# Order of work in the first attention stage of a two-block layer: projections as filling, gates and pa's products moved

## The reference, cut to what matters

```python
z = h @ w_in                      # fq fk fv ff dq dk dv ga gb
log_f = log_sigmoid(ff + b_fgate)
o_a = fox_attention(fq, fk, fv, log_f)        # 8 heads of 64, causal, bias F_q - F_k (F = cumsum(log_f))
o_b = rms_norm(diff_attention(dq, dk, dv))    # 4 heads: softmax(q1 k1) - lam * softmax(q2 k2), v of 128
y = sigmoid(ga + b) * (o_a @ w_pa) + sigmoid(gb + b) * (o_b @ w_pb)
x = x + y @ w_o
```

## Time and profile before

| | |
|---|---|
| median of three runs | 1101.2 us (1100.53 to 1102.28) |
| profiled execution: its own time | 1100.98 us |
| its span, first to last instruction | 1099.2 us |
| mean granted TensorE clock | 0.965 of 2.4 GHz |
| busy: PE, DVE, ACT, POOL | 93%, 36%, 34%, 13% of the span |
| first block's mixer, until the last matmul of wo1 | to about 254 us |
| routing and experts | to about 760 us |
| second block | to the end |

### The profile page before, as it was taken

The page is one execution under the profiler, slowest core; times in us unless marked ns, Lnnn a source line. Parts: engine busy times, 40 slices in busy tenths (PEclk is TensorE's granted clock), DMA queues, the critical chain, the costliest instruction groups (busy, mean ns, idle before and its releaser), DMA issues.

```text
span 1099.2 us, 14880 instructions
## 1 busy us (share of the span) xinstructions
PE 1019.1 (93%) x6333; PEld 713.8 (65%) x6333; DVE 391.3 (36%) x753; ACT 370.7 (34%) x610; POOL 138.1 (13%) x87
## 2 busy tenths in 40 slices
PE   7999999887999999998989999886999999999996
PEld 6996779866544444433334333335898999999995
DVE  3444335454312121211111101214433443683464
ACT  5444555543011111111111111014345564655342
POOL 1110011322000000000000000001312102242123
PEclk8998999889999999999999999898899999999999
DMA  8964666347599999999999999996264554554400
GB/s 294 345 240 151 230 220 249 146 180 306 188 421 420 419 420 420 419 418 421 419 419 420 419 419 419 419 404 229 90 216 169 176 175 154 187 179 172 173 1 38
DMA packets 83003, 307.92 MB, mean 280 GB/s; under 512 B 6607, under 2 KB 11112, under 8 KB 58352
## 3 DMA queue, kind: packets, MB, share of 16 engines
q1 hardware_dynamic: 79144, 302.16, 70.2%
q10 hardware_dynamic: 3784, 4.73, 1.3%
HBM read 305.81 MB, written 2.63 MB: 281 GB/s over the span
## 4 chain that ended last, share of the span: by engine, by line
PE 71%; DMA 10%; DVE 7%; SPq 4%; ACT 4%; issue 2%; POOL 1%; ACTq 0%; POOLq 0%; DVEq 0%
PE bank L722 69%; DMA arena<-in_w 5%; DMA ring<-in_w 5%; SPq L774 4%; DVE arena L1184 2%; DVE arena L1187 2%; DVE arena L1190 1%; DVE wR L1184 1%; PE bank L1133 1%; ACT wR L1732 1%; ACT arena L1903 1%; POOL wR L2067 1%; PE bank L906 1%; PE bank L900 0%; POOL small L2055 0%
## 5 line engine op out<-in xcount | busy, mean ns | idle before, releaser
L722 PE MATMUL bank<-hTR,wR 128*128 128x256 f32 x2520 | 316.6, 287 | 5.1 <-DVE wR L1184 2.0
L722 PEld LDWEIGHTS bank<-hTR,wR 128*128 128x128 f32 x2520 | 309.1, 194 | 8.7 <-issue 7.2
L722 PE MATMUL bank<-ring,arena 128*64 128x512 f32 (+1 forms) x1056 | 228.7, 602 | 9.5 <-DMA ring<-in_w 9.4
L1732 ACT ACTIVATE wR<-ring 128x1024 fp32r<-128x1024 f32 x161 | 168.2, 1053 | 119.2 <-PE bank L722 117.2
L1184 DVE TENSOR_TENSOR wR<-ring,wR 128x1024 fp32r<-128x1024 f32 x121 | 153.0, 1271 | 151.6 <-ACT wR L1732 151.4
L722 PE MATMUL bank<-arena 128*64 128x512 f32 (+8 forms) x778 | 171.8, 549 | 12.3 <-DMA arena<-in_w 6.3
L722 PEld LDWEIGHTS bank<-ring,arena 128*64 128x64 f32 (+1 forms) x1056 | 69.3, 136 | 141.9 <-issue 129.0
L2067 POOL TENSOR_TENSOR wR<-ring,wR 128x1024 fp32r<-128x1024 f32 x40 | 97.3, 2431 | 387.3 <-ACT wR L1732 387.3
L1184 DVE TENSOR_TENSOR arena<-arena,bank 128x256 f32<-128x256 f32 (+1 forms) x36 | 16.0, 450 | 363.7 <-ACT arena L1903 358.1
L1882 ACT ACTIVATE arena<-bank 64x512 f32<-64x512 f32 x64 | 37.9, 593 | 307.9 <-PE bank L722 307.5
L722 PEld LDWEIGHTS bank<-arena 128*64 128x64 f32 (+4 forms) x778 | 67.4, 154 | 100.2 <-issue 82.8
(11 more groups left out here) (204 smaller groups left out, 846.8 us busy)
## 6 DMA issues: line engine op xcount, KB each, us to landing
ring<-in_w SPq DMA_DIRECT2D x120, 1024.0 KB, 25.1
arena<-in_w SPq DMA_DIRECT2D x72, 1024.0 KB, 25.5
ring<-in_w_in SPq DMA_DIRECT2D x30, 2048.0 KB, 8.9
ring<-in_w_ada SPq DMA_DIRECT2D x6, 2048.0 KB, 8.0
ring<-in_w_o SPq DMA_DIRECT2D x2, 2048.0 KB, 11.6
ring<-in_w_o_attn SPq DMA_DIRECT2D x2, 2048.0 KB, 7.8
ring<-in_w_o_conv SPq DMA_DIRECT2D x2, 2048.0 KB, 7.8
ring<-in_w_out SPq DMA_DIRECT2D x2, 2048.0 KB, 9.1
```

The costliest lines, as they stand in the source:

```text
L722: return pe.e.matmul(o, l, r, start=start, stop=stop)
L1732: eng.activation(h, w, ACT.Copy).then_inc(s_high, 1)
```

## The change

- dq and dk go into the filling: dq's two halves are drawn from it before the loop (the first, then `cumsum`, then the second), dk in rounds 0 and 1, dv in rounds 2 and 3.
- Only `bf` 0 stands in front of the loop. `bf` 1, 2 and 3 are in rounds 0, 2 and 4, behind that round's `qk`.
- `ada` i stands in the filling in front of gate projection i, 4 and 5 behind g3. Every round takes two units of filling until round 15; it runs out there. The order of loads is changed to fit (g1 before ada2, and so on).
- pa's four pieces leave the filling: they run in rounds 16 and 17 and behind the loop, among the last differential head's steps. Their gates are made beside them.
- pa's product is no longer copied from PSUM by ACT and multiplied by POOL: DVE multiplies bank and gate into `PA` in one instruction. The sigmoids of all four quarters stand in front of the pb loop.
- `outer_pe` waits for each head's output at the first product that reads it, not for all four in front.

```diff
-        chunks += [ada[0], gate[0], ada[1], ada[2], gate[1], ada[3], gate[2], ada[4], gate[3], ada[5]]
+        chunks += [ada[0], gate[0], ada[1], gate[1], ada[2], gate[2], ada[3], gate[3], ada[4], ada[5]]
...
-        project(O1, "dq", "h1")
-        PB.use("zT", 7)
-        PB.use("cum", 7)
-        O1.add("cumsum")
-        project(O1, "dk", "h1")
-        O1.add("rbuf")
-        for hp in range(4):
-            PB.use(("bf", hp), SR.next())
-            O1.add("bf", hp)

         def fill_first():
+            for nm in ("dq", "dk"):
+                for c2 in range(2):
+                    u = PB.use((nm, c2), PR.next())
+                    for st in O1.pair(nm, c2, u, "h1"):
+                        O1.add(*st)
+                        if st[3] == 0:
+                            yield
+                    O1.add("evict", nm, c2)
+                    yield
...
+            def ada_step(i):
+                u = PB.use(("adaw", i), PR.next())
+                O1.add("ada", i)
+                O1.loads.release(f"ada{i}")
+                yield
+                PB.use(("ada", i), u.bank)
+                O1.add("ada_sum", i)
+
             for g in range(4):
+                yield from ada_step(g)
                 for c2 in range(2):
...
-            for jj in range(4):
-                u = PB.use(("pa", jj), PR.next())
-                i_ = O1.take("pa")
-                done_by(i_, u)
-                O1.add("outer", i_, "pa", jj)
-                O1.add("evict", "pa", jj)
-                yield
+            for i in (4, 5):
+                yield from ada_step(i)
...
         fill = fill_first()
+        for _ in range(2):
+            next(fill)
+        PB.use("zT", 7)
+        PB.use("cum", 7)
+        O1.add("cumsum")
+        for _ in range(2):
+            next(fill)
+        O1.add("rbuf")
+        PB.use(("bf", 0), SR.next())
+        O1.add("bf", 0)
...
-            ada_sum()
-            next(fill, None)
-            if i in (0, 4, 5, 7, 9, 12):
-                ada_step()
+            if i < 6 and i % 2 == 0:
+                PB.use(("bf", i // 2 + 1), SR.next())
+                O1.add("bf", i // 2 + 1)
+            if i < 16:
+                next(fill, None)
+            elif i == 16:
+                for _ in fill:
+                    pass
+                pa_outer(0)
             if job:
                 PB.use(("pt", n_pt), TR.next())
                 O1.add("p_turn", n_pt, *job)
...
-            if i in (6, 9, 11, 12, 13, 14, 15):
+            if i < 16:
                 next(fill, None)
-        while late:
-            next(fill, None)
-            h = late.pop(0)
-            PB.use(("dt", h), U_["do", h].bank)
-            O1.add("diff_turn", h)
-        for _ in fill:
-            pass
+            elif i == 16:
+                O1.add("gate", 0)
+                O1.add("evict", "pa", 0)
+                pa_outer(1)
+        O1.add("gate", 1)
+        O1.add("evict", "pa", 1)
+        pa_outer(2)
+        PB.use(("dt", 3), U_["do", 3].bank)
+        O1.add("diff_turn", 3)
+        O1.add("gate", 2)
+        O1.add("evict", "pa", 2)
+        pa_outer(3)
+        O1.add("gate", 3)
+        O1.add("evict", "pa", 3)
         for jj in range(4):
-            O1.add("gate", jj)
             u = PB.use(("pb", jj), PR.next())
...
-            for m in range(4):
-                emptied(pe, U_["fo" if nm == "pa" else "dt", m])
             for s in range(2):
                 for k in range(4):
+                    emptied(pe, U_["fo" if nm == "pa" else "dt", k])
...
+                    elif nm == "pa":
+                        u = U_["pa", c2]
+                        filled(v, u)
+                        v.wait_ge(s_gate, c2 + 1)
+                        emptied(v, U_["s", 7])
+                        tt(flat2(PA, 2 * c2), banks[u.bank][:, :], flat2(gates, 2 * c2), ALU.mult).then_inc(u.free, 1)
...
-                        eng.activation(flat2(PA, 2 * c2), banks[u.bank][:, :], ACT.Copy).then_inc(u.free, 1)
...
-                    eng.tensor_tensor(flat2(PA, 2 * jj), flat2(PA, 2 * jj), flat2(gates, 2 * jj), ALU.mult).then_inc(s_pag, 1)
```

More of the change, by code:

```diff
@@ L362, in bass_two_hybrid_blocks @@
                              "drs", "dsq"))
-        s_siluc, s_gate, s_pag, s_ysum, s_yh, s_shift, s_rexp, s_ss, s_rrow, s_rbuf, s_sca = (
-            sem(n) for n in ("siluc", "gate", "pag", "ysum", "yh", "shift", "rexp", "ss", "rrow", "rbuf", "sca"))
+        s_siluc, s_gate, s_ysum, s_yh, s_shift, s_rexp, s_ss, s_rrow, s_rbuf, s_sca = (
+            sem(n) for n in ("siluc", "gate", "ysum", "yh", "shift", "rexp", "ss", "rrow", "rbuf", "sca"))
         s_gA, s_ag, s_aTh, s_uz, s_conv, s_cb, s_cg, s_cTh, s_msum, s_mh, s_fg = (
@@ L496, in fill_first, with pa_outer @@
                     yield
-            for jj in range(4):
-                u = PB.use(("pa", jj), PR.next())
-                i_ = O1.take("pa")
-                done_by(i_, u)
-                O1.add("outer", i_, "pa", jj)
-                O1.add("evict", "pa", jj)
-                yield
-        fill = fill_first()
[L506 to L521, removed]
+            for i in (4, 5):
+                yield from ada_step(i)
+        def pa_outer(jj):
+            u = PB.use(("pa", jj), PR.next())
+            i_ = O1.take("pa")
+            done_by(i_, u)
+            O1.add("outer", i_, "pa", jj)
+        fill = fill_first()
+        for _ in range(2):
[8 more added lines that the diff above has]
+        O1.add("bf", 0)
         late, out_of = [], []
@@ L566, in bass_two_hybrid_blocks @@
                 n_pt += 1
-            if i in (6, 9, 11, 12, 13, 14, 15):
+            if i < 16:
                 next(fill, None)
-        while late:
-            next(fill, None)
-            h = late.pop(0)
-            PB.use(("dt", h), U_["do", h].bank)
-            O1.add("diff_turn", h)
-        for _ in fill:
-            pass
+            elif i == 16:
[7 more added lines that the diff above has]
+        O1.add("diff_turn", 3)
+        assert late == [3] and not out_of
+        O1.add("gate", 2)
[3 more added lines that the diff above has]
+        O1.add("evict", "pa", 3)
         for jj in range(4):
-            O1.add("gate", jj)
             u = PB.use(("pb", jj), PR.next())
@@ L584, in bass_two_hybrid_blocks @@
         O1.add("y", 3)
-        assert ada_next[0] == 6 and not ada_full
         O1.add("x_again")
@@ L1349, in first_steps @@
                     emptied(v, u)
-                    v.wait_ge(s_pag, jj + 1)
+                    emptied(v, U_["pa", jj])
                     tt(T, T, flat2(PA, 2 * jj), ALU.add).then_inc(s_ysum, 1)
@@ L1770, in first_steps @@
                         last.then_inc(u.free, 1)
-                    elif nm == "pa":
-                        u = U_["pa", c2]
-                        filled(s, u)
-                        emptied(s, U_["s", 7])
-                        eng.activation(flat2(PA, 2 * c2), banks[u.bank][:, :], ACT.Copy).then_inc(u.free, 1)
                 elif what == "ada":
@@ L2078, in first_steps @@
                     rsqrt(st[:, 4:6], st[:, 2:4], s_drs)
-                elif what == "gate":
-                    jj = a[0]
-                    emptied(p, U_["pa", jj])
-                    p.wait_ge(s_gate, jj + 1)
-                    eng.tensor_tensor(flat2(PA, 2 * jj), flat2(PA, 2 * jj), flat2(gates, 2 * jj), ALU.mult).then_inc(s_pag, 1)
             def second_norm():
```

## The result

The changed kernel takes 1092.19 us (median of 6 runs, 1091.67 to 1095.31), the kernel before 1101.41 on the same chip (6 runs, 1098.67 to 1103.02): ratio 0.9925, 95% interval [0.9907, 0.9943]. That is about 9 us faster by the medians and 8.3 by the ratio (6.3 to 10.2 by its interval). The forecast was 1.4, and its range ended at 1094.5. The profiled execution took 1091.67 us for a span of 1089.9, at a mean granted clock of 0.972.

The account below looks back on a forecast made before the run. Loads bound the expert stage, whose start waits for PE through the mixer. A gain of 0.9 us until the first pb product ended plus net 0.5 behind it made 1.4: 1099.8 us, range 1094.5 to 1105.

Parts of the forecast that it names:

- The bound of the stage: Expert stage: DMA at full share, 1.01 at 416 GB/s, so it lasts as long as its bytes take.
- So whatever the mixer gains or loses passes to the end one for one: From the first expert's refill at 283.46 on: the refill waits for PE, so mixer gains reach the end unchanged.
- The waits of the mixer: PE's idle time up to the first pb product: 9.4 us in the new order against 10.6 before.
- Clock in the mixer: Low clock up to the first pb product: round 0 certain at 2.6; cumsum, rounds 4 and 16 together 4.0 us.
- From the first pb product to wo0: Chain from that product's end to wo0's third piece: 19.4 us instead of 22.1, without sigmoids and POOL's multiplications.
- The low clock at wo0: At the start of wo0's third piece: clock low after PE idles, costing 2.2 us ahead of 72 matmuls without a wait.
- Sum of the mixer: Whole mixer: 0.9 gained until the first pb product has ended, net 0.5 from there, together 1.4 us.
- The rule of the table load: ACT's sigmoid table load: 1.28 us by the row; the skill's added 1.38 drain would make the gain 0.5, not 1.4.
- Exchange: Mixer, the forecast itself: waits and clock give back nearly what goes, 1099.8 us (1098 to 1102.5); chance 0.42.
- The clock holds: Cumsum, round 4 and round 16 keep 2.4 GHz, 4.0 us come back: 1095 to 1096 us; chance 0.34.
- DVE held up: Loop rounds 11, 13, 15: PE waits on DVE's splits queued behind POOL's rsqrt, 1104.5 to 1106 us; chance 0.2.
- the loads decide: In the loop: a chunk comes late, each 2 MB taking about 5 us; chance 0.04, to either side.

Follow-up runs that it names:

- d_before: Kernel before with eleven identity matmuls, about 2.3 us, added in front of the first expert: 1099.29 us, ratio 0.9988.
- k_before: Kernel before with 6 and 4 identity matmuls that end inside PE's waits at the end of the expert stage: 1095.52 us, ratio 0.9945.
- k_after: Changed kernel with 6 and 4 identity matmuls that end inside PE's waits at the end of the expert stage: 1092.89 us, ratio 0.9925.
- d_after: Changed kernel with eleven identity matmuls, about 2.3 us, added in front of the first expert: 1096.43 us, ratio 0.9955.
- h_after: Changed kernel with 13 and 9 identity matmuls at PE's waits in experts 28 to 31, longer than those waits: 1100.14 us, ratio 1.0004.
- h_: Kernel before and changed kernel, each with 13 and 9 identity matmuls at PE's waits in experts 28 to 31: 1104.01 and 1100.14 us.
- d_: Kernel before and changed kernel, each with eleven identity matmuls in front of the first expert: 1099.29 and 1096.43 us.
- k_: Kernel before and changed kernel, each with 6 and 4 identity matmuls inside waits late in the expert stage: 1095.52 and 1092.89 us.
- The held pair: Kernel before and changed kernel, each with 6 and 4 identity matmuls inside waits late in the expert stage: ratios 0.9945 and 0.9925.
- the three edits: Changed kernel with cumsum behind dq's third tile, `bf` 3 in round 3, pa's first piece ahead of `diff_turn` 2: 1087.82 us, ratio 0.9887.

## Why the prediction was wrong

**The bound of the stage (right).** The experts' loads pace PE for 409.3 to 409.8 us behind the refill in every profile in which PE waits for the last chunk. More traffic or another order of loads decided nothing; after the change PE waits for no DMA between 66 and 240 us.

**"So whatever the mixer gains or loses passes to the end one for one" (the step that failed).** It holds only as far as the last wait for a chunk. From there PE is the bound again for about 60 us of experts and for the second block, and how long these take depends on where the clock falls: 55.6 to 60.3 us for one and the same tail, 342.7 to 346.2 from there to the end. The prediction put these stages at nothing without a reason: it looked for low clock only between 60 and 240 us, where the change was, and none of its rivals has a price for it behind the mixer. The row at 692 us was in the same profile: 10.04 us for 32 matmuls that take 7.09 elsewhere, behind waits of 1.72 and 1.32. A kernel before that is caught there can win 4 us from any change that moves it; `d_before` won 3.8 there from a delay. `k_before` shows what carries it: 5.5 of the 9 us come back with fillers alone, 3.3 of them in the tail by its profile. Why the clock falls there in one order and not in the other stays open: the waits in front are the same, 1.72 and 1.32.

**The waits of the mixer (right).** Forecast idle 9.4 us, measured 2.38 + 1.59 + 1.73 + 1.04 + 2.02 = 8.8, and 0.30 at the last head's norm. The covers held: no wait on the probabilities and none on the gates. DVE's waits in order for POOL's rsqrt, 14.0 us in three before, are 9.4 with a longest of 4.0 after, and none reached PE:

```profile
DVE arena L1202 <- POOL small L2071: 9.4, 3, 4.0
```

**Clock in the mixer (places right, the sum by luck).** All five low stretches fell where they were charged. The four ahead of the pb products were priced at 2.6 + 4.0 = 6.6 together; at half of PE's busy time in each they cost 1.70 + 1.75 + 1.70 + 1.51 = 6.7. That the sums agree is luck: the ledger had one at 2.6 and three at 2.2 with six chances in ten each, and there came four at about 1.7. When the changed kernel was repeated, two of them were twice as long, with nothing changed. To the start of the first pb product the prediction's working gives a loss of 1.0 (old 17.4 less the 1.9 of that product, new 16.5). From the table load in front of `forget` the profile of before takes 153.4; the changed kernel's takes 152.6, as in `k_after` and `d_after`, and 155.3 when repeated and in `h_after`, where the clock is low for 6.8 us each at cumsum and round 0. So 0.8 gained or 1.9 lost; the ledger's loss of 1.0 lies between.

**From the first pb product to wo0 (right).** Forecast 3.0 for that product at full clock and a chain of 19.4, together 22.4, against 26.9 before. Measured 234.49 - 211.62 = 22.9, and 22.5 to 23.0 in the other four profiles.

**The low clock at wo0 (mis-sized).** It was charged with 2.2 us on top. It came (233.9 to 237.4), but from wo0's third piece to the refill the time is 46.4 against 46.2: before, the clock fell at 258.5 and again at 275.6 us, after only at 257.8. The charge should have been made against what that stage lost anyway.

**Sum of the mixer (too small).** The forecast was 1.4. Over five profiles of each kind (plain, repeated and the `h_`, `d_` and `k_` ones, the delay of 2.3 taken off) the time from the table load to the refill is 226.8 on average before and 222.9 after: 3.9. Of that, 0.2 is lost up to the first pb product (forecast: 1.0 lost), 4.4 gained from there to wo0's third piece (4.5), and 0.3 lost behind it (2.2). The held pair gives 2.2 by the ratios. So it was forecast too small by about 2.5 us, most of it the charge at wo0. Alone that would have meant a time of 1097 to 1099, inside the range.

**The rule of the table load (went by the row, right).** Timeline of ACT in the changed kernel:

```profile
202.29 1.28 ACT L1855 ACT_TABLE_LOAD   x1
203.59 1.15 ACT L1855 ACTIVATE arena<-arena 128x512 f32<-128x512 f32 x2
```

The sigmoids begin 0.02 us behind the load, and `diff_turn` 3 waits 0.30. The Trainium skill (ScalarE: Activation LUTs, What ACT_TABLE_LOAD costs) adds a drain of 1.38 us, by which about 0.9 was to be expected there; the trace does not show it.

**The rivals.** "Exchange" had the right waits and the wrong end. "The clock holds" came nearest in time, for the wrong reason: the clock did not hold in the mixer, it held at 692 us. "DVE held up" and "the loads decide" did not happen.

## What to carry to other kernels

When a stage paced by loads stands behind the change, a gain passes through it unchanged, but only to the last wait for a load. Read what PE does behind that point too, and look there for matmuls that take longer than their like. Where PE waits twice for 1 to 2 us in a row, the clock may or may not fall, and a change anywhere ahead of it redraws that lot: price it on both sides of the range, in the kernel before as well. A few idle matmuls that end inside such a wait took the lot out of that place, and here they gave the kernel before 5.5 us at no cost; use them on both kernels before judging an edit by a few us. They hold no other place: the second block drew its own lot, worth 2 to 3 us. The best version here is the change with the three edits and the fillers: 1086.9 us, 0.9874 of the kernel before.

## What the runs showed of the hardware that was not expected

- The same program, waiting for the same things, is granted low clock in different places from run to run: cumsum's wait of 2.39 us was followed by 6.8 us at 1.2 GHz in one profile and by 3.4 in another. The Trainium skill (TensorE: Matmul & The Clock Gate, What's actually happening) says that the activity window behind the gate is free-running and does not start anew with the kernel; the spread of 1090.3 to 1103.6 us in 12 runs of the changed kernel, at granted clocks from 0.974 to 0.957, agrees with that, though no run here shows the cause.
- A delay can be harmless: 2.3 us of work added ahead of the experts left the kernel before as fast or made it up to 2.8 us faster, [0.9975, 1.0000], and made the changed one 3.6 slower.
- The waits that cost the clock were short, 1.72 and 1.32 us with about 1.5 us of narrow matmuls between them; with all but 0.19 of the first and 0.9 of the second filled, it was 1.00 there in each of three kernels. Only for the kernel before does that say something: the other two were at 1.00 there in their first profiles too, with the waits unfilled.
- Two low stretches of 6.8 us behind the experts come with 346.1 to 346.2 us from the tail to the end in seven profiles, whichever order the mixer has; the other eight, with less of PE's work at low clock there, take 342.7 to 344.9.
- What stays open is what decides where the clock falls. No run here held it in the second block, and the gain of the mixer alone is known only to about 2 us.
